# Where large SBUF buffers begin: multiples of 512 bytes, and 64 bytes over for one family of matmul operands

## The reference

```python
# first layer: mixer (SSD half and attention half) and MLP
h = rmsnorm(x, g_mix) @ w_in                       # 2048 -> about 5,700 columns
x = x + concat(ssd(h), indexed_attention(h)) @ w_out
x = x + square(relu(rmsnorm(x, g_mlp) @ w_up)) @ w_down      # 2048 -> 8192 -> 2048
# second layer: attention with a forget bias, and MLP
h = softmax(q k^T * s + c_t - c_s) v @ fox_w_out   # q, k, v from norm(x) @ fox_w_in
x = x + rmsnorm(h)
x = x + rmsnorm(square(relu(rmsnorm(x) @ mlp_w1)) @ mlp_w2)
```

## Time and profile before

| | |
|---|---|
| median of 3 runs | 2267.22 us (2264.46 to 2267.34) |
| the profiled execution, its own time | 2267.66 us |
| its span, first to last instruction | 2265.9 us |
| TensorE matmuls | 11,798, busy 2232.0 us |
| mean granted TensorE clock | 0.995 |

### The profile page before, as it was taken

The page is one execution under the profiler, slowest core; times in us unless marked ns, Lnnn a source line. Parts: engine busy times, 40 slices in busy tenths (PEclk is TensorE's granted clock), DMA queues, the critical chain, the costliest instruction groups (busy, mean ns, idle before and its releaser), DMA issues. The chain is left out here.

```text
span 2265.9 us, 27606 instructions
## 1 busy us (share of the span) xinstructions
PE 2232.0 (99%) x11798; PEld 1899.8 (84%) x11798; DVE 1313.1 (58%) x1541; ACT 990.0 (44%) x1117; POOL 26.4 (1%) x71
## 2 busy tenths in 40 slices
PE   9999999999999999999999999999999999999998
PEld 8988778988888888887898888888888888888876
DVE  5688664555544466776455554546555444667754
ACT  6453554444433344544344434534445333444432
POOL 1000000000000000000001000000000000000000
PEclk9999999999999999999999999999999999999999
DMA  7455445566555566665557555555765556666664
GB/s 240 148 168 167 140 137 192 173 186 188 189 192 193 187 186 186 188 202 178 180 167 213 163 181 161 174 189 162 215 194 188 185 187 189 191 191 190 193 235 148
DMA packets 280985, 415.46 MB, mean 183 GB/s; under 512 B 13284, under 2 KB 167056, under 8 KB 280608
## 3 DMA queue, kind: packets, MB, share of 16 engines
q1 hardware_dynamic: 279376, 409.89, 56.5%
q0 software_dynamic: 1456, 3.81, 0.7%
q10 hardware_dynamic: 32, 0.01, 0.0%
HBM read 409.47 MB, written 4.21 MB: 183 GB/s over the span
## 5 line engine op out<-in xcount | busy, mean ns | idle before, releaser
L1123 DVE TENSOR_TENSOR wl<-raw,wh 128x2048 fp32r<-128x2048 f32 x376 | 860.2, 2290 | 494.8 <-ACT wh L605 493.3
L605 ACT ACTIVATE wh<-raw 128x2048 fp32r<-128x2048 f32 x376 | 719.4, 1916 | 531.4 <-DMA raw<-in_mlp_w_dram 169.5
L2012 PE MATMUL bank<-XHL,wh 128*128 128x512 f32 x2368 | 829.9, 393 | 0.0
L2014 PE MATMUL bank<-XHL,wl 128*128 128x256 f32 x2368 | 666.4, 281 | 0.0
L2012 PEld LDWEIGHTS bank<-XHL,wh 128*128 128x128 f32 x2368 | 444.2, 188 | 99.7 <-issue 0.2
L2014 PEld LDWEIGHTS bank<-XHL,wl 128*128 128x128 f32 x2368 | 446.0, 188 | 0.4
L1985 PE MATMUL bank<-wh,hh 128*128 128x512 f32 x768 | 301.9, 393 | 5.1 <-DVE wl L1123 5.1
L1987 PE MATMUL bank<-wh,hl 128*128 128x512 f32 x768 | 303.4, 395 | 0.0
L1986 PE MATMUL bank<-wl,hh 128*128 128x512 f32 x768 | 303.3, 395 | 0.0
L1985 PE MATMUL bank<-wh,XHL 128*128 128x512 f32 x576 | 231.2, 401 | 1.3 <-DVE XHL L1131 1.3
L1987 PE MATMUL bank<-wh,XHL 128*128 128x512 f32 x576 | 228.3, 396 | 0.0
(11 more groups left out here) (396 smaller groups left out, 1832.4 us busy)
## 6 DMA issues: line engine op xcount, KB each, us to landing
raw<-in_mlp_w_dram SPq DMA_DIRECT2D x128, 1024.0 KB, 5.4
raw<-in_w_up_dram SPq DMA_DIRECT2D x64, 1024.0 KB, 5.5
raw<-in_w_down_dram SPq DMA_DIRECT2D x64, 1024.0 KB, 5.1
raw<-in_fox_w_in_dram SPq DMA_DIRECT2D x48, 1024.0 KB, 5.4
raw<-in_w_in_dram SPq DMA_DIRECT2D x40, 1024.0 KB, 5.0
raw<-in_w_out_dram SPq DMA_DIRECT2D x16, 1024.0 KB, 5.1
raw<-in_fox_w_out_dram SPq DMA_DIRECT2D x16, 1024.0 KB, 5.1
raw<-in_w_in_dram SPq DMA_DIRECT2D x16, 256.0 KB, 6.9
```

The source lines that it names most:

```text
L605: act.activation(wh[:, j, :, :], raw[:, j, :, :], ACT.Copy).then_inc(hi_ready, 1)
L1123: dve.tensor_tensor(wl[:, j, :, :], raw[:, j, :, :], wh[:, j, :, :].bitcast(F32), ALU.subtract)\
L2012: pe.matmul(bk[:, :].rearrange("p (s t) -> p s t", s=2), sh, XHL[:, k, :, :], start=k == 0, stop=False, skip_group_check=True)
L2014: mm = pe.matmul(bk[:, 0:TOK], sl, XH[:, k, :], start=False, stop=k == KT - 1, skip_group_check=True)
```

## The change

`wh` moves from the head of SBUF into the arena, behind `XHL`. The arena begins at a multiple of 512 bytes. `XHL` (with `TH`/`TL`, which share its bytes) begins 64 bytes past a multiple of 512; `wh`, `raw` and `wl` at a multiple. `hh`, `hl`, `RB`, `G`, `G1` and the g combinations begin 64 bytes over, `FK`, `FV` and what follows don't. Sizes, instructions, waits and their order stay.

```diff
+LINE = 512
+BESIDE = 64
...
-        wh = sb("wh", [P, 4, 4, 512], F32R)
...
-        arena = -(-nc.sbuf_base // 32) * 32
+        def lined_up(at):
+            return -(-at // LINE) * LINE
+
+        arena = lined_up(nc.sbuf_base)
...
         combinations(arena, "x", 4)
-        arena = region(arena, [("X", [P, NT, D], F32)])
+        arena = region(arena, [("X", [P, NT, D], F32)]) + BESIDE
         low = region(arena, [("TH", [P, 3, 512], F32R)])
         region(low, [("TS", [P, 3, 512], F32)], [("TL", [P, 3, 512], F32R)])
         arena = region(arena, [("XHL", [P, KT, 2, TOK], F32R)])
-        X, XHL, TH, TS, TL = (T[n] for n in "X XHL TH TS TL".split())
+        arena = region(lined_up(arena), [("wh", [P, 4, 4, 512], F32R)])
+        X, XHL, TH, TS, TL, wh = (T[n] for n in "X XHL TH TS TL wh".split())
...
         at = region(arena, [("HB", [P, NT, D], F32)], [("FQ", [P, HEADS_F, TOK], F32)])
+        at += BESIDE
         low = region(at, [("hh", [P, HT, TOK], F32R), ("hl", [P, HT, TOK], F32R), ("RB", [P, 2, 512], F32)])
         combinations(low, "g", 1)
         region(low, [("G", [P, D], F32)])
 
         region(at, [("G1", [P, D], F32)])
+        at -= BESIDE
         at = region(at, [("FK", [P, HEADS_F, TOK], F32)])
```

## The result

The change makes the kernel slower: 2276.81 us against 2266.6 us for the kernel before, six runs each, ratio 1.0049 with a 95% interval of 1.0034 to 1.0064. The forecast was 2221 us, range 2205 to 2287, faster with chance 0.60.

A forecast was written before the change was run, and what follows sets the result against it. The prediction took TensorE's stream of matmuls, busy 99% of the span, to bound the kernel. Savings of 21.3, 23.6 and 6.6 us made 51.5, less a tenth 46: 2267.2 - 46 = 2221 us, range 2205 to 2287.

The forecast's parts named there:

- The excess: Time each float32r matmul takes over its columns at 2.4 GHz: 11 to 19 ns, over 11,500 matmuls, all addresses can touch.
- The step that failed: All four matmul forms: operands uniform modulo 64 let the whole stream settle at the quick pace, together 51.5 us.
- The term of 23.6 us saved for `rows` and `three`: `rows` and `three`: 4620 matmuls go from 232.2 to 227.1 ns, saving 23.6 us.
- that of 21.3 us for the pairs: `half_cols`: 2368 pairs of matmuls each lose 9.0 ns from 349.3, saving 21.3 us.
- that of 6.6 us for `k_tile`: `k_tile`: 4.3 ns less for each of 3 x 512 matmuls, saving 6.6 us.
- The two quick stretches: In `seven` and `NHm`/`NLm`, 227 and 113.3 ns a matmul, put down to operands all 32 bytes over multiples of 64.
- That a stretch needs time or luck to settle: Uniform stretches settle late: 24 matmuls for `NHm`, up to six in `seven`, over 48 for `NHf`.
- a tenth taken off for settling: Whole stream: deduction for stretches after a wait, transpose or side work, taking the 51.5 us saving to 46 us.
- The rival of the collision: Weight loads at an offset unequal to the streaming operand's cost time; 37 us slower, 2304 us; chance 0.22.
- the additional third: In `rows`, loads at unequal offset go from two of three to all, costing 2.6 ns x 4620, 12.0 us.
- The rule of the Trainium skill: TensorE has two independent read ports, so relative offsets are worth nothing and the time stays at 2267 us.
- The rival of no effect: Quick stretches come from instruction order, not addresses, so the time stays at 2267 us; chance 0.18.

The follow-up runs named there:

- x32: Kernel after with `XHL` at 32 bytes past a multiple of 64 and `wh`, `wl`, `raw`, `hh`, `hl` on one: 2247.59 us, ratio 0.9912.
- shift32: Kernel before with 32 unused bytes ahead of `wh`, every relative offset kept: 2265.62 us, ratio 0.9995.
- same480: Kernel after with every large buffer at 480 modulo 512: 2252.85 us, ratio 0.9942.
- beside0: Kernel after without its 64 bytes, all large buffers on multiples of 512: 2252.12 us, ratio 0.9938.
- the pace kernels: Kernels running TensorE alone with the kernel's matmul forms copied and the operands' offsets varied, each run once; `rows` took 226.8 ns at (0,0,0).
- the grid: TensorE alone, 64 stretches: `XHL` at 0, high (`wh`) and low (`wl`) each at 0 to 224 by 32; pairs at (0,64,0) 350.1 ns.
- pace4: TensorE alone: pairs at five offset sets (x, high, low: `XHL` or `hh`, `wh`, `wl`), 0 to 7 short matmuls ahead; 63 steps at (0,0,0) took 21.9 and 22.3 us.
- the map: Paces by offsets (x, high, low: `XHL` or `hh`, `wh`, `wl`) from running TensorE alone; pairs at (0,64,0) 340.2 ns.
- only_x: Kernel after with the 64 bytes kept under `XHL` alone: 2256.1 us, ratio 0.9954.
- only_hh: Kernel after with the 64 bytes kept under `hh`, `hl`, `RB` and `G` alone: 2265.94 us, ratio 0.9997.
- pace5: TensorE alone: `rows` with `XHL` at 0, 64, 128, 192 and 128 to 16 stationary columns, then plain fp32; 0-to-64 difference 6.7 ns at 128 columns.
- pace3: TensorE alone, 64 stretches: `XHL` at 0, every pair of high and low offsets from 0 to 224 by 32; pairs at (0,192,0) 340.0 ns.
- pace2: TensorE alone, 50 stretches: one of three offsets at a time moved through 0 to 480 by 32, others at 0; `rows` at (480,128,480) 232.2 ns.

## Why the prediction was wrong

- *What bounds the kernel.* Right. In every variant the time follows the pace of TensorE, and the other engines' work stayed hidden; in the kernel after and in `x32` TensorE has no new wait over 0.6 us. The excess lay over 11,138 float32r matmuls, not 11,500, which changes nothing in the sum.
- *The step that failed* is "Modulo 64 every operand of the four forms is then at 0, with nothing mixed. If uniformity is what the settled pace needs, the whole stream can settle". Uniformity modulo 64 is not what it needs. `shift32` and `same480` against `beside0` show that only the offset of one operand from the other counts, and the pace kernels that it counts modulo 256. The change sets `XHL` and `hh` 64 past the weights, where `rows` takes 233.3 ns; before, `wh` lay 160 past them modulo 256 and `wl` at the same offset, with 232.2 ns. For pairs it left the one pace before, 349.3 ns, for two, 353.3 and 348.9. The term of 23.6 us saved for `rows` and `three` is 5.1 us lost; that of 21.3 us for the pairs is 7.2 us lost; that of 6.6 us for `k_tile` is 1.1 us saved.
- *The two quick stretches* were read rightly as quick, and the common cause put on them was wrong. `TH` with `hh` was at equal offsets, and equal offsets give `rows` 226.7 ns. But equal offsets for a few matmuls are not enough. `TH` with `CH` was equal as well and took 231.5 ns in the second `seven`; in the kernel after `TH` with `hh` is still equal (both at 64), and the three take 229.9 ns from start to start in the mean (`TH` with `hl` lasts 392 ns in the rows above, and lasted 389). Where everything around them is equal too, in `beside0`, all of these take 226.7. The pieces of `NHm` lie 64 or 192 bytes past `XHL` modulo 256; in the grid `k_tile` has 113.6 to 113.9 ns at high and low (64,64), (64,192) and (192,64), but 117.8 at (192,192), where every second piece is. The `narrow` form was not run by itself, so its quick half stays open.
- *That a stretch needs time or luck to settle* was nearer than the rest: more than one pace exists at one set of offsets, and what ran ahead decides. The two paces of pairs in the kernel after, 353.3 and 348.9 ns, are those of (64,0,0) in `pace4`, and a stretch keeps either for eight panels and more; so a tenth taken off for settling was no measure of anything.
- *The rival of the collision* had the right sign and much of the mechanism for `rows`: equal offsets are the good case, 226.8 ns. It put 7.7 ns on each unequal load; `wh` and `wl` both 160 past the other operand, which is (96,0,0) in the map, cost 234.2 - 226.8 = 7.4. What it had wrong is that 64 apart costs less, 6.5 (233.3), so the additional third came to 1.1 ns a matmul and not 2.6. For pairs it took equal offsets to be free and quickest, at 340.3 ns, and they are at 346.7 or 353.3; it put 9.0 ns more a pair where 3.05 was measured. So its 37 us were too many. The windows hold 851 and 687 matmuls, where it would have had 840 and 683.
- *The rule of the Trainium skill* (TensorE: Matmul & The Clock Gate, Step-by-step: what each phase is for), that loading weights takes no bandwidth from the running matmul, is not borne out here for float32r: with the same matmuls, moving one operand by 64 bytes costs 6.7 ns on 226.7, and the cost goes with the number of weight columns. That the weight load causes it is the likeliest reading and is not shown. For plain fp32 the trace agrees with the rule, 429.2 ns a record both times.
- *The rival of no effect* is dead: `beside0` takes 24.7 us off by the 64 bytes alone, and `only_x` and `only_hh` split the loss in `rows` into its two parts. Their times don't add up to it, 4.0 + 13.8 = 17.8 us, since against `beside0` the pairs are 1.3 and 4.1 us quicker in the halves and only 0.6 with both, and `k_tile` 5.0 and 1.4 and with both 4.2.

Left open: where the period of 256 bytes comes from, and why a pace keeps itself up. A clash of TensorE's two reads in SBUF would fit the offsets, the period and the shrinking with the columns, but no run shows it, and it does not say why a full load at offset 0 (226.7 ns) is quicker than one of 16 columns (231.7). Whether offsets at a finer grain than 32 bytes do better than `x32` wasn't tried in the kernel.

## What to carry to other kernels

In this kernel, whose time is a stream of float32r matmuls with a weight load for each, the SBUF offset of the moving operand from the stationary one, modulo 256 bytes, is worth 1.3% of the time (2276.8 against 2247.6 us) and up to 4% of the pace of `rows` and of pairs, and the best value depends on the form; it is cheap to map with a kernel that runs TensorE alone. Measure each form several times with different work just ahead, and take an offset whose pace is the same at all of them rather than one that was quickest once: (0,64,0) had 340 ns in some stretches and 350 or 353 in others, and (32,0,0), 346.7 to 346.9 each time, made the better kernel. Alignment to 64 or 512 bytes as such bought nothing.

## What the runs showed of the hardware

- With 128 stationary columns, 512 moving float32r columns take 226.7 to 235.5 ns at the clock level of 2.4 GHz, by offsets alone (`pace5`, `pace3`). A plain fp32 matmul of 512 columns shows as two records of 429.2 ns each, 2.5 ns over two cycles a column, at both offsets tried, 0 and 64 (`pace5`).
- The dependence of `rows` and `k_tile` on the offsets has a period of 256 bytes (`pace2`). The pace of `rows` with the kernel's banks is the same with and without other engines and DMA, and does not hang on where in SBUF the buffers lie (226.8 ns in `beside0` and `same480`, 226.7 to 227.3 in `pace2`).
- With 16 stationary columns the pace is 231.7 ns at all four offsets, with 32 it is 230.5 to 231.7: worse than with 128 at the right offset (226.7) and better than with 128 at a wrong one (233.4).
- The same instructions can settle at two or three paces, up to 4% apart (340.3, 350.0 and 353.4 ns a pair), and keep one for the rest of a stretch of 64 pairs, 22 us (`pace4`).
